# A decoder step's input projection: four items at a time, 512 prompt columns per matmul, sample tokens as the stationary operand

## The chip, the core and the metric

The program runs on one core of a Trainium2 chip. TensorE (PE) multiplies, VectorE (DVE) and ScalarE (ACT) work elementwise, GpSimd (POOL) does a few set-up operations, and SyncE (SP) issues most of the DMA transfers. The metric is the device time of one execution in microseconds. The kernel is compared with itself after one change to its first stage.

## What is computed

One decoder layer is applied to 512 prompt tokens and to 64 sample tokens (8 sequences of 8). The first stage, which the change concerns, is the RMS norm and one combined projection whose columns are then split:

```python
def mixer_inputs(x, norm_w, w_in, a_q_norm, a_k_norm):
    xn = rms_norm(x, norm_w)
    u, o, mz, ig, fg, q, kv, g, az = jnp.split(xn @ w_in, SPLIT_AT, axis=-1)
    q = rms_norm(q.reshape(B, T, A_HEADS, A_DH), a_q_norm)
    ...                       # the two key parts of kv get their own head norms
    g = jax.nn.sigmoid(g)
```

`x` has 2048 features. `u` goes through a causal convolution of four taps and a SiLU (x times its sigmoid); `o` gets a sigmoid; `z` and `az` get a SiLU; values, `o` and `z` are turned so that tokens lie on partitions. The mLSTM heads, the sparse attention of prompt and samples, the output projection and a gate follow. They are the same text in both kernels.

## The kernel before

Every stage is a block of its own, with a barrier between two stages. `project_in` is the first stage. Tokens lie on the free axis: T = 576 columns, the 512 of the prompt (TP) and then the 64 of the samples (TSA). The projection's outputs are cut into 53 **items** of 128 output features: 4 cmp, 4 key, 8 q, 1 gate, 4 val, 8 u, 8 o, 8 z, 8 az, in this order (`ITEMS`).

Each product is made of three in a rounded 32-bit type (F32R): x is split into `x_hi + x_lo`, a weight into `w_hi + w_lo`, and `w_hi·x_hi + w_hi·x_lo + w_lo·x_hi` is summed. An item has 16 contraction steps `k`. Its weights come in two halves of 8 steps (load, `w_hi` by ACT in `high`, `w_lo` by DVE in `low`, L381), in rings of three. For each step the three products are done on two column halves of 288, so an item has 96 matmuls (L250), each with its own weight load. An item's 576 columns occupy two of PSUM's banks, and three items go round in `mm`; two more banks (`aux`) serve the side work of PE.

The order on each engine is written out by hand. PE runs item s and then `aside(s - 1)`: a head norm's column sums (L218), or turns (L232). It starts item s when item s-3 has left PSUM (`evac`). On DVE, in step s: `low(2s + 2)`, `evacuate(s - 1)` (PSUM times the token's 1/rms, L417 or L408 to L410), `second(s - 2)`, `first(s - 1)`, `low(2s + 3)`. `low(m)` waits for `w_hi(m)` and for the matmuls of half m-3. ACT has `high`, the exponentials of the sigmoids (`first`, L312 to L314) and the head norms' powers (`second`). SP has the loads, and the stores of finished items.

At the start the four chunks of x arrive, ACT makes `x_hi`, DVE makes `x_lo` (L480), then ACT squares x and DVE adds the squares over `k` (L489). PE sums them over partitions behind item 1 (L257), which waits for the last addition, and ACT makes `rstd` of it. Nothing is evacuated before `rstd` is ready.

Of the kernel before, what the change touches and what calls it, by code (L numbers as in the profile page):

```python
# [14 lines left out]
P = 128  # L15
# [74 lines left out]
class Buffers:  # L90
# [3 lines left out]
ITEMS = ([("cmp", n) for n in range(4)] + [("key", n) for n in range(4)] + [("q", n) for n in range(8)] + [("gate", 0)]  # L94
         + [("val", n) for n in range(4)] + [(kind, n) for kind in ("u", "o", "z", "az") for n in range(8)])
NI = len(ITEMS)
NORMED, GATED = ("key", "q"), ("u", "o", "z", "az")
# [8 lines left out]

def project_in(nc, B, a, o):

    HALF, HK, RING = T // 2, KD // 2, 3
    STORED = ("cmp", "key", "val", "u", "az")  # L110
    halved = lambda ap: ap.rearrange("p (x t) -> p x t", x=2)
    with Semaphores(nc) as sem, ExitStack() as ctx:
        sb = lambda n, s, d=F32: ctx.enter_context(nc.sbuf_tensor(n, s, d, side="right"))
        ps = lambda n, s: ctx.enter_context(nc.psum_tensor(n, s, F32))
        xhi, xlo = sb("x_hi", [P, KD, T], F32R), sb("x_lo", [P, KD, T], F32R)
        raw = sb("w_raw", [P, RING, HK, P])
        whi, wlo = sb("w_hi", [P, RING, HK, P], F32R), sb("w_lo", [P, RING, HK, P], F32R)
        stg = sb("p_stage", [P, 3, T])
# [10 lines left out]
        mm = ps("mm", [P, 3, 2, CH])  # L129
        aux = ps("aux", [P, 2, CH])  # L130
        x_in = [sem(f"x_in{i}") for i in range(4)]
        w_in = [sem(f"w_in{i}") for i in range(RING)]
# [5 lines left out]
        whi_done, wlo_done, half_done, evac = sem("whi_done"), sem("wlo_done"), sem("half_done"), sem("evac")  # L138
# [3 lines left out]
        kv_out, row_out = [sem(f"kv_out{i}") for i in range(3)], sem("row_out")  # L142
# [5 lines left out]
        def _(sp):  # L148
            def load(m):
                if m >= 2 * NI:  # L150
                    return
                if m >= RING:
                    sp.wait_ge(wlo_done, m - RING + 1)
                sp.dma_start(raw[:, m % RING], a["w_in"][m]).then_inc(w_in[m % RING], 16)

            def store(j):
                kind, n = ITEMS[j]
                if kind in STORED:
# [6 lines left out]
                    src = stg[:, j % 3, :]  # L165
# [14 lines left out]
                    sp.dma_start(dst, src).then_inc(kv_out[j % 3], 16)  # L180
# [6 lines left out]
            for i in range(4):  # L187
                sp.dma_start(x[:, 4 * i:4 * i + 4, :], a["x_fm"][:, 4 * i:4 * i + 4, :]).then_inc(x_in[i], 16)
                if i < RING:
                    load(i)  # L190
            for s in range(NI + 2):
                load(2 * s + 3)
                load(2 * s + 4)
                if s >= 2:
                    store(s - 2)
                if 4 <= s < 4 + NB:
# [6 lines left out]
        def _(pe):  # L203
# [31 lines left out]
            for s in range(NI + 1):  # L235
# [23 lines left out]
                if s >= 1:  # L259
                    aside(s - 1)  # L260
# [2003 lines left out]
```

## Time and profile of the kernel before

| | us |
|---|---|
| median of 3 runs (2226.57 to 2228.03) | 2227.49 |
| the profiled execution | 2227.76 |
| its span from the first to the last instruction | 2226.1 |
| `project_in`, from the span's start to the next stage's first instruction | 725.5 |

In the page's busy times PE has 2051.2 us (92%), DVE 830.4 (37%), ACT 697.4 (31%), POOL 50.7 (2%). A row of the timeline gives start, length, engine, line, operation, output and inputs, the count of like instructions merged into it, and in brackets the idle time before it and what ended it. A merged row is as long as from the first start to the last end. Matmuls overlap: the distance of two starts is what one costs. So do the operations of DVE and ACT by some 0.1 us. A row of the windows gives, for a stretch, each engine's busy time with its number of instructions, then the granted TensorE clock (1.00 is 2.4 GHz, 0.50 is 1.2 GHz), the DMA share and GB/s.

### The profile page before, as it was taken

To read this page: it belongs to the slowest core of one execution; us is meant where nothing else is said; L and a number is where in the kernel's file an instruction comes from. 1 tells how busy PE (TensorE), PEld (TensorE's weight loads), DVE (VectorE), ACT (ScalarE), POOL (GpSimd) and SP (SyncE) were. 2 spreads that over 40 slices of the span, in tenths; PEclk is the share of its full clock that TensorE was granted. 3 is DMA by queue.
4 is the path that set the end of the run, shared out by engine and by line. 5 is a ranking of instruction groups with operands and counts; after the bars stand their busy time and mean duration, and the time that the engine had idled before them with its cause. 6 is when DMAs were issued, how large, how long until landed. Compare 5 with 4: busy or idle time off the path is not lost. (4 is left out here: it accounts for less than half of the span.)

```text
span 2226.1 us, 34268 instructions
## 1 busy us (share of the span) xinstructions
PE 2051.2 (92%) x13409; PEld 1658.3 (74%) x13409; DVE 830.4 (37%) x1639; ACT 697.4 (31%) x1328; POOL 50.7 (2%) x99
## 2 busy tenths in 40 slices
PE   7999999999999799968997799999997699999998
PEld 7999999999999455655554354544444599989997
DVE  6233235423332334526563134433334422242332
ACT  6332223333332222205663223332222321142222
POOL 0000000000000100000000000000000011100000
PEclk9999999999999788858998899999997799999999
DMA  5452233333331433220123768888864642223320
GB/s 190 163 187 79 87 98 98 107 102 107 99 112 53 155 140 140 82 106 29 58 75 128 262 221 277 294 298 301 301 243 152 228 147 77 81 86 107 99 73 22
DMA packets 163699, 315.00 MB, mean 142 GB/s; under 512 B 18893, under 2 KB 68430, under 8 KB 160466
## 3 DMA queue, kind: packets, MB, share of 16 engines
q1 hardware_dynamic: 143656, 278.98, 37.2%
q10 hardware_dynamic: 19882, 33.83, 4.3%
q8 instruction: 107, 1.75, 0.3%
q14 instruction: 54, 0.44, 0.1%
HBM read 280.75 MB, written 40.26 MB: 144 GB/s over the span
## 5 line engine op out<-in xcount | busy, mean ns | idle before, releaser
L250 PE MATMUL mm<-x_hi,w_hi 128*128 128x288 f32 x1696 | 368.3, 299 | 14.2 <-DVE w_lo L381 14.2
L250 PE MATMUL mm<-x_hi,w_lo 128*128 128x288 f32 x1696 | 363.9, 296 | 0.0
L250 PE MATMUL mm<-x_lo,w_hi 128*128 128x288 f32 x1696 | 363.8, 296 | 0.0
L250 PEld LDWEIGHTS mm<-x_hi,w_hi 128*128 128x128 f32 x1696 | 274.4, 189 | 15.8 <-issue 12.5
L250 PEld LDWEIGHTS mm<-x_hi,w_lo 128*128 128x128 f32 x1696 | 273.9, 189 | 0.0
L250 PEld LDWEIGHTS mm<-x_lo,w_hi 128*128 128x128 f32 x1696 | 273.8, 189 | 0.0
L381 DVE TENSOR_TENSOR w_lo<-w_raw,w_hi 128x1024 fp32r<-128x1024 f32 x106 | 129.8, 1225 | 384.8 <-ACT w_hi L280 384.8
L1515 PE MATMUL s_pH<-wide,cw_sample 128*128 128x512 f32 x512 | 244.5, 619 | 16.2 <-DMA wide<-pages 13.7
L1997 PE MATMUL o_mm<-o_feat_hi,o_w_hi 128*128 128x288 f32 x1024 | 224.7, 301 | 23.6 <-DVE o_feat_lo L2072 19.4
L1997 PE MATMUL o_mm<-o_feat_lo,o_w_hi 128*128 128x288 f32 x1024 | 221.0, 298 | 0.0
L1997 PE MATMUL o_mm<-o_feat_hi,o_w_lo 128*128 128x288 f32 x1024 | 220.7, 297 | 0.0
L280 ACT ACTIVATE w_hi<-w_raw 128x1024 fp32r<-128x1024 f32 x106 | 112.1, 1058 | 342.8 <-PE mm L250 342.7
L1515 PEld LDWEIGHTS s_pH<-wide,cw_sample 128*128 128x128 f32 x512 | 94.4, 196 | 133.3 <-issue 115.7
L1997 PEld LDWEIGHTS o_mm<-o_feat_hi,o_w_hi 128*128 128x128 f32 x1024 | 167.8, 191 | 26.3 <-issue 22.6
L1997 PEld LDWEIGHTS o_mm<-o_feat_lo,o_w_hi 128*128 128x128 f32 x1024 | 166.7, 191 | 0.0
L1997 PEld LDWEIGHTS o_mm<-o_feat_hi,o_w_lo 128*128 128x128 f32 x1024 | 166.6, 190 | 0.0
L2066 DVE TENSOR_TENSOR o_w_lo<-o_w_raw,o_w_hi 128x2048 fp32r<-128x2048 f32 x32 | 73.4, 2293 | 113.6 <-ACT o_w_hi L2027 113.6
L1753 ACT ACTIVATE s_scores<-s_scores,s_mx 128x512 f32<-128x512 f32 (+1 forms) x72 | 48.3, 671 | 115.4 <-DVE s_mx L1868 114.8
L1626 PE MATMUL s_pO<-s_kv,s_probT 128*64 128x128 f32 x1024 | 70.0, 279 | 4.7 <-DVE s_probT L1874 4.6
L1329 ACT ACTIVATE a_p<-a_pS,a_nmax 128x128 f32<-128x128 f32 (+3 forms) x128 | 66.2, 524 | 16.8 <-DVE a_nmax L1368 16.8
L2027 ACT ACTIVATE o_w_hi<-o_w_raw 128x2048 fp32r<-128x2048 f32 x32 | 60.8, 1900 | 24.3 <-DMA o_w_raw<-w_out 24.3
L1600 PE MATMUL s_pS<-s_kv,qblk 128*64 128x512 f32 x256 | 65.6, 626 | 1.1 <-DVE s_mx L1863 0.8
(402 smaller groups left out, 2296.3 us busy)
## 6 DMA issues: line engine op xcount, KB each, us to landing
wide<-pages SPq DMA_DIRECT2D x256, 256.0 KB, 3.6
w_raw<-w_in SPq DMA_DIRECT2D x106, 512.0 KB, 3.9
s_kv<-pages SPq DMA_DIRECT2D x128, 256.0 KB, 11.1
s_kv<-pages ACTq DMA_DIRECT2D x128, 256.0 KB, 8.1
o_w_raw<-w_out SPq DMA_DIRECT2D x16, 1024.0 KB, 8.6
o_w_raw<-ple_gate SPq DMA_DIRECT2D x16, 1024.0 KB, 6.7
m_state<-state SPq DMA_DIRECT2D x4, 2056.0 KB, 12.8
state_sample<-m_state SPq DMA_DIRECT2D x4, 2056.0 KB, 6.6
```

Of the source, the lines that this page charges most:

```text
L250: last = nc.tensor.matmul(mm[:, s % 3, y, 0:HALF], w[:, m % RING, kk, :], f[:, k, y * HALF:(y + 1) * HALF], start=k == 0 and i == 0, stop= ...
L280: s_.activation(whi[:, m % RING], raw[:, m % RING], ACT.Copy).then_inc(whi_done, 1)
L381: v.tensor_tensor(wlo[:, m % RING], raw[:, m % RING], whi[:, m % RING].bitcast(F32), ALU.subtract).then_inc(wlo_done, 1)
L1329: s_.activation(prob[:, d % 2, g2, 0:(qt + 1) * P], pS[:, d % 2, g2, 0:(qt + 1) * P], ACT.Exp, bias=nmx[:, d, g2:g2 + 1], accum_out=rs[:, ...
L1515: last = mm(pH[:, x, :], cw1[:, x, k, :], comp[:, HP * cc:HP * cc + HP, k * 64 + x * 32:k * 64 + x * 32 + 32], start=k == 0, stop=k == 7)
L1600: last = mm(pS[half(gp), j % 2, :], B.qblk[:, gp, b, :], kvp[:, 4 * j:4 * j + 4, gp * P:(gp + 1) * P], start=True, stop=True)
L1626: last = mm(pO[half(gp), 0, 0:P], probT[:, q % 2, i, half(gp)], kvp[:, 4 * q + i, v0:v0 + P], start=q == 0 and i == 0, stop=False)
L1753: s_.activation(chunk(j), chunk(j), ACT.Exp, bias=mx[:, 11:12], accum_out=rs[:, j:j + 1]).then_inc(p_ready, 1)
L1997: last = nc.tensor.matmul(mm[:, j % 2, x, 0:HALF], w[:, j % 2, k, :], f[:, k, cols], start=k == 0 and i == 0, stop=k == KD - 1 and i == 2)
L2027: s_.activation(whi[:, j % 2], raw[:, c % 2, :, (j % 2) * P:(j % 2 + 1) * P], ACT.Copy).then_inc(whi_done, 1)
L2066: v.tensor_tensor(wlo[:, j % 2], raw[:, (j // 2) % 2, :, (j % 2) * P:(j % 2 + 1) * P], whi[:, j % 2].bitcast(F32), ALU.subtract).then_inc( ...
```

## The change

The items stay in their order. They are grouped: `GROUPS` has 14 groups, 13 of four items and the gate alone. A group of four is done in 8 **units** of two contraction steps each, the gate in two units of eight, 106 units in all. A unit holds the weights of all four items for its two steps: 512 KB, as a half item did.

- **Prompt columns.** In a unit each of the four items has 2 steps x 3 products = 6 matmuls on all 512 prompt columns, into its own PSUM bank (`mm` has four). All four banks are finished in the group's last unit, and there is no fifth.
- **Sample columns.** The samples' x (128 stationary columns: their `x_hi` beside their `x_lo`) is loaded as weights, and the 512 output features of the group stream past it, into one bank `tail`; `w_lo` has 64 stationary columns. That is 4 matmuls of 512 columns per unit. Behind the group ACT copies `tail` to `sums` (`summed`), PE adds the two halves and turns the result back with four matmuls against `stack` (`fold`), and DVE scales the 4 x 64 columns (`sample`). The gate's samples stay moving: 48 matmuls of 64 columns.
- **Rings.** `w_hi` has three places, `w_lo` two (`LO = 2`), so `low(m)` now waits for unit m-2. The stage buffer `stg` has five places instead of three.
- **Order.** `lanes()` lays the steps of an item out over slots, one slot per unit. With `end` the slot of the group's last unit: four `prompt` at `end`, `fold` at `end + 1`, four `sample` at `end + 2`, and for item i `first` at `end + 2i + 2`, `aside` one later, `second` two later, `store` three later (six slots later still for the gate). In a slot ACT and DVE do `high(s + 2)` or `low(s + 2)` first, and then the entries, an older group's ahead of a younger one's. The convolution has moved from the evacuation to `first`.
- **Start.** `x_lo` covers the prompt alone, and DVE makes the samples' `x_lo` with a second instruction per `k`. The sum of squares on PE stands behind unit 2 and no longer behind item 1.

```diff
+GROUPS = ([[("cmp", n) for n in range(4)], [("key", n) for n in range(4)], [("q", n) for n in range(4)], [("q", n) for n in range(4, 8)],
+           [("gate", 0)], [("val", n) for n in range(4)]]
+          + [[(kind, 4 * x + n) for n in range(4)] for kind in ("u", "o", "z", "az") for x in range(2)])
...
+            def unit(m):
+                g, c = UNITS[m]
...
+                pe.wait_ge(whi_done, m + 1)
+                pe.wait_ge(wlo_done, m + 1)
+                for i in range(n):
+                    if c == 0 and g:
+                        free = start_of(g - 1) + min(i + 1, len(GROUPS[g - 1]))
+                        pe.wait_ge(prompt_out, free)
+                    own = slice(i * P, (i + 1) * P)
+                    for kk, k in enumerate(ks):
...
+                        for y, (w, x) in enumerate(((hi, xhi), (hi, xlo), (lo, xhi))):
+                            last = nc.tensor.matmul(mm[:, i, :], w[:, kk, own], x[:, k, 0:TP], start=k == 0 and y == 0, stop=k == KD - 1 and y == 2)
+                    if final:
+                        last.then_inc(item_done, 1)
...
+                        if wide:
+                            last = nc.tensor.matmul(tail[:], xhi[:, k, TP:T + TSA], hi[:, k % 2, :], start=k == 0, stop=k == KD - 1)
+                        else:
+                            last = nc.tensor.matmul(tail[0:TSA, :], xhi[:, k, TP:T], lo[:, k % 2, :], start=False, stop=False)
...
+                last.then_inc(unit_done, 1)
...
             def low(m):
...
-                if m >= RING:
-                    dve.wait_ge(half_done, m - RING + 1)
+                if m >= LO:
+                    dve.wait_ge(unit_done, m - LO + 1)
...
-            for s in range(1, NI + 2):
-                if s >= 2:
-                    low(2 * s + 2)
-                if s <= NI:
-                    evacuate(s - 1)
-                if s >= 2:
-                    second(s - 2)
-                if s <= NI:
-                    first(s - 1)
-                low(2 * s + 3)
+            for s in range(2, LAST + 1):
+                low(s + 2)
+                for what, j in LANES.get(s, []):
+                    if what == "prompt":
+                        prompt(j)
...
```

How the instructions now stand, at three places. On DVE where the last u item meets the first o item, before (L433 and L434 are the convolution, L468 the SiLU's product, L381 `low`, L417 the evacuation):

```order
L433 SCALAR_TENSOR_TENSOR p_stage<-upad,convw,p_stage 128x512 [waits p_dve_step]
L434 SCALAR_TENSOR_TENSOR p_stage<-upad,convw,p_stage 128x64
L468 TENSOR_TENSOR p_stage<-p_stage,p_square 128x576 [waits sig_ready]
L381 TENSOR_TENSOR w_lo<-w_raw,w_hi 128x1024 [waits half_done,whi_done] x2
L417 TENSOR_TENSOR p_stage<-mm,p_rstd 128x576 [waits kv_out2,half_done]
L381 TENSOR_TENSOR w_lo<-w_raw,w_hi 128x1024 [waits half_done,whi_done] x2
```

The same place of the change (L532 and L533 are the convolution of the last u item, L569 its product, L502 the prompt's evacuation, L470 `low`, L517 the samples' scaling):

```order
L532 SCALAR_TENSOR_TENSOR p_stage<-upad,convw,p_stage 128x512 [waits p_dve_step]
L533 SCALAR_TENSOR_TENSOR p_stage<-upad,convw,p_stage 128x64
L569 TENSOR_TENSOR p_stage<-p_stage,p_square 128x576 [waits sig_ready]
L502 TENSOR_TENSOR p_stage<-mm,p_rstd 128x512 [waits kv_out4,item_done]
L502 TENSOR_TENSOR p_stage<-mm,p_rstd 128x512 [waits kv_out0,item_done]
L502 TENSOR_TENSOR p_stage<-mm,p_rstd 128x512 [waits kv_out1,item_done]
L502 TENSOR_TENSOR p_stage<-mm,p_rstd 128x512 [waits kv_out2,item_done]
L470 TENSOR_TENSOR w_lo<-w_raw,w_hi 128x1024 [waits unit_done,whi_done] x2
L517 TENSOR_TENSOR p_stage<-p_turned,p_rstd 128x64 [waits fold_done] x4
```

The four evacuations of a group stand together, behind the convolution of an item of the group before and behind that slot's `low`.

On PE between two items before, with the head norm's sums between them:

```order
L250 MATMUL mm<-x_hi,w_lo 128x288 x2
L218 MATMUL aux<-p_square,p_pair 128x288 [waits sq_ready,aux_read]
L218 MATMUL aux<-p_square,p_pair 128x288
L250 MATMUL mm<-x_hi,w_hi 128x288 [waits evac,wlo_done,whi_done]
L250 MATMUL mm<-x_hi,w_hi 128x288
```

On PE between two groups of the change, the last unit of the one and the first matmuls of the next:

```order
L302 MATMUL mm<-x_hi,w_lo 128x512
L317 MATMUL p_tail<-w_lo,x_hi 64x512 x2
L315 MATMUL p_tail<-w_hi,x_hi 128x512 x2
L302 MATMUL mm<-x_hi,w_hi 128x512 [waits prompt_out,wlo_done,whi_done]
L302 MATMUL mm<-x_lo,w_hi 128x512
```

The wait `evac` was for an item three back; `prompt_out` is for the group that ended on the row above. At the end of that first unit, before the second:

```order
L302 MATMUL mm<-x_hi,w_lo 128x512
L315 MATMUL p_tail<-w_hi,x_hi 128x512 [waits sums_ready]
L315 MATMUL p_tail<-w_hi,x_hi 128x512
L317 MATMUL p_tail<-w_lo,x_hi 64x512 x2
L281 MATMUL p_turned<-p_stack,p_sums 128x64 [waits evac,sums_ready]
L281 MATMUL p_turned<-p_stack,p_sums 128x64 x3
L302 MATMUL mm<-x_hi,w_hi 128x512 [waits wlo_done,whi_done]
```

The four matmuls of L281, each 64 columns of full 32-bit, have come onto PE's queue, once per group of four.

## Rows read from the trace of the kernel before

**Rows 1.** Windows: busy time and count per engine, granted clock, DMA share.
```profile
12.40:16.50 4.10, 4.00 (x17) 4.04 (x18) 4.10 (x6) 3.33 (x5) 0.00 (x0) 1.00 0.88 324
...
40.00:718.70 678.70, 676.83 (x5055) 673.40 (x5054) 235.01 (x335) 209.98 (x262) 0.00 (x0) 1.00 0.34 108
718.70:725.50 6.80, 0.00 (x0) 0.00 (x0) 1.40 (x2) 2.05 (x3) 0.01 (x1) 0.85 0.11 43
725.50:732.00 6.50, 0.00 (x0) 0.00 (x0) 4.85 (x10) 2.05 (x3) 5.64 (x22) 0.50 0.83 297
732.00:737.00 5.00, 4.92 (x6) 2.19 (x7) 4.79 (x7) 0.60 (x1) 0.00 (x0) 0.50 1.05 346
```

**Rows 2.** Timeline of PE, two rows 17 contraction steps apart.
```profile
687.98 0.43 PE L250 MATMUL mm<-x_hi,w_hi 128*128 128x288 f32 x2
...
701.59 0.42 PE L250 MATMUL mm<-x_hi,w_hi 128*128 128x288 f32 x2
```

**Rows 3.** Timeline in the next stage: full 32-bit matmuls of 512 and 64 columns.
```profile
737.63 0.19 PEld L686 LDWEIGHTS m_pj<-m_ch,m_qkv_w 128*128 128x128 f32 x1 [0.24 <-issue]
738.06 0.19 PEld L686 LDWEIGHTS m_pj<-m_ch,m_qkv_w 128*128 128x128 f32 x1 [0.24 <-issue]
...
741.49 1.90 PE L694 MATMUL m_nm<-m_ch,m_qkv_w 128*128 128x64 f32 x16
```

**Rows 4.** Timeline of DVE around one u item.
```profile
340.11 1.23 DVE L381 TENSOR_TENSOR w_lo<-w_raw,w_hi 128x1024 fp32r<-128x1024 f32 x1 [2.55 <-ACT w_hi L280]
341.25 0.45 DVE L408 TENSOR_TENSOR upad<-mm,p_rstd 128x288 f32<-128x288 f32 x1
...
341.91 0.22 DVE L410 TENSOR_TENSOR upad<-mm,p_rstd 128x64 f32<-128x64 f32 x1
342.27 0.55 DVE L430 TENSOR_SCALAR p_stage<-upad,convw,convb 128x512 f32<-128x512 f32 x1
...
348.17 0.76 DVE L468 TENSOR_TENSOR p_stage<-p_stage,p_square 128x576 f32<-128x576 f32 x1 [2.18 <-ACT p_square L314]
```

**Rows 5.** Timeline of DVE: `second` of a q item, and of an o item.
```profile
152.35 0.57 DVE L453 SCALAR_TENSOR_TENSOR qblk<-p_stage,qnw,p_rk 64x64 f32<-64x64 f32 x2
152.94 0.75 DVE L455 SCALAR_TENSOR_TENSOR landing<-p_stage,qnw,p_rk 128x512 f32<-128x512 f32 x1
...
431.52 0.68 DVE L461 COPY p_rows<-aux 128x512 f32<-128x512 f32 x1
432.12 0.27 DVE L462 COPY p_rows<-aux 64x128 f32<-64x128 f32 x1
```

**Rows 6.** Timeline of the start, DVE's rows.
```profile
8.25 3.01 DVE L480 SCALAR_TENSOR_TENSOR x_lo<-landing,normw,x_hi 128x576 fp32r<-128x576 f32 x4 [6.54 <-ACT x_hi L349]
11.18 1.22 DVE L381 TENSOR_TENSOR w_lo<-w_raw,w_hi 128x1024 fp32r<-128x1024 f32 x1
...
19.28 1.22 DVE L381 TENSOR_TENSOR w_lo<-w_raw,w_hi 128x1024 fp32r<-128x1024 f32 x1
...
37.73 1.22 DVE L381 TENSOR_TENSOR w_lo<-w_raw,w_hi 128x1024 fp32r<-128x1024 f32 x1
```

**Rows 7.** The same start on PE: its first matmul, and the sum of squares.
```profile
12.49 0.82 PE L250 MATMUL mm<-x_hi,w_hi 128*128 128x288 f32 x2 [12.49 <-DVE w_lo L381]
...
40.09 1.13 PE L257 MATMUL aux<-p_rk,ones 128*128 128x288 f32 x4
```

**Rows 8.** Timeline of all engines at the end of `project_in`.
```profile
718.12 0.42 PE L250 MATMUL mm<-x_hi,w_lo 128*128 128x288 f32 x2
...
718.58 0.76 DVE L417 TENSOR_TENSOR p_stage<-mm,p_rstd 128x576 f32<-128x576 f32 x1 [9.09 <-PE mm L250]
719.37 0.68 ACT L312 ACTIVATE p_square<-p_stage 128x576 f32<-128x576 f32 x1 [10.68 <-DVE p_stage L417]
...
722.30 0.32 SPq L180 DMA_DIRECT2D az_scratch<-p_stage  x1
725.49 0.34 SPq L621 DMA_DIRECT2D m_qkv_w<-m_w  x1
```

More of the change, by code:

```diff
@@ L104, in nth, with lanes, put @@
     return sum(1 for kind, _ in ITEMS[:j + 1] if kind in kinds)
-def project_in(nc, B, a, o):
-    HALF, HK, RING = T // 2, KD // 2, 3
+def lanes():
+    at = {}
+    def put(slot, what, j):
+        at.setdefault(slot, []).append((what, j))
+    base = 0
+    for g, group in enumerate(GROUPS):
+        end = max(v for v, (x, _) in enumerate(UNITS) if x == g)
+        gate = group[0][0] == "gate"
+        for i in range(len(group)):
+            put(end, "prompt", base + i)
+        if not gate:
+            put(end + 1, "fold", g)
+            for i in range(len(group)):
+                put(end + 2, "sample", base + i)
+        for i in range(len(group)):
+            x = end + 2 * i + (8 if gate else 0)
+            put(x + 2, "first", base + i)
+            put(x + 3, "aside", base + i)
+            put(x + 4, "second", base + i)
+            put(x + 5, "store", base + i)
+        base += len(group)
+    return at
+def project_in(nc, B, a, o):
+    RAW, HI, LO, SLOTS = 3, 3, 2, 5
+    LANES = lanes()
+    LAST = max(LANES) + 1
+    FOLDS = [g for g, group in enumerate(GROUPS) if len(group) == 4]
+    start_of = lambda g: sum(len(group) for group in GROUPS[:g])
+    group_of = lambda j: max(g for g in range(len(GROUPS)) if start_of(g) <= j)
+    nfold = lambda g: FOLDS.index(g) + 1
     STORED = ("cmp", "key", "val", "u", "az")
-    halved = lambda ap: ap.rearrange("p (x t) -> p x t", x=2)
     with Semaphores(nc) as sem, ExitStack() as ctx:
@@ L254, in _ @@
+            for s in range(LAST + 1):
+                if s < NU:
+                    unit(s)
+                if s == 2:
                     pe.wait_ge(ones_ready, 1)
                     pe.wait_ge(added, KD - 1)
-                    for y in range(2):
-                        last = nc.tensor.matmul(aux[:, y, 0:HALF], B.ones[:], rk[:, y * HALF:(y + 1) * HALF], start=True, stop=True)
+                    for part, out in both(rk):
+                        last = nc.tensor.matmul(out, B.ones[:], part, start=True, stop=True)
@@ L357, in _ @@
                     high(3)
[L358 removed]
             act.wait_ge(ssq_done, 1)
[L360 removed]
+            for part, read in both(rstd):
+                last = s_.activation(part, read, ACT.Ln, bias=B.eps[:, 0:1], scale=1.0 / D)
+            step(last)
             s_.activation(rstd[:], rstd[:], ACT.Exp, scale=-0.5).then_inc(rs_ready, 1)
[L362 to L368 removed]
+            for s in range(2, LAST + 1):
+                high(s + 2)
+                for what, j in LANES.get(s, []):
+                    if what == "fold":
+                        summed(j)
+                    elif what == "first":
+                        first(j)
+                    elif what == "second":
+                        second(j)
         @block.vector
@@ L491, in _ @@
                     low(3)
-            low(4)
             dve.wait_ge(small_in, 16 * SMALL)
```

227 lines of the change are left out of this document (134 added, 93 removed).

## The prediction

> **What bounds the kernel now.** Read the windows first [rows 1]. From 40 to 718.7 us PE is busy for 676.83 of 678.70 us at a granted clock of 1.00; DVE and ACT are busy for a third of it. So `project_in` is bound by PE alone: what lies on PE's queue is paid in full, and DVE or ACT cost nothing unless PE comes to wait for them. The other stages are untouched. Next comes the distance of two matmuls. From 687.98 to 701.59 us lie 17 contraction steps, 102 matmuls with nothing between them [rows 2]: 13.61 / 102 = 0.1334 us each. 288 columns at 2.4 GHz are 0.1200 us, so 0.0134 us of each is something else. At the start, at 1.2 GHz, two take 0.48 us: 17 in the 4.1 us of the first window [rows 1], 0.24 us each, which is just the columns.
>
> **Matmuls.** Before: 53 x 96 = 5088, x 0.1334 = 678.7 us. The change has 104 units x 28 = 2912 matmuls of 512 columns, and 48 in the gate: 2960, plus 48 of 64 columns. Columns in all hardly differ (5088 x 288 = 1.465 million, 2960 x 512 + 48 x 64 = 1.519 million); what can be won is the 0.0134 us, 2128 times fewer. No rounded 32-bit matmul of 512 columns is in the trace. Its bounds come from two sides. Upper: the excess grows with the columns, 0.1334 x 512 / 288 = 0.2372 us. Lower: a full 32-bit one goes over the array twice, and each pass of 512 columns takes 738.06 - 737.63 = 0.43 us for 1024 column times [rows 3], 0.2133 x 2 with 0.003 over: so 0.2153 us for a single pass without the excess. Between them: the excess is fixed per matmul, 0.2133 + 0.0134 = 0.2267. I take this, since at 1.2 GHz, where a matmul lasts twice as long, none of it shows, while a share of the column time would. The 48 of 64 columns take 0.112 us each: 16 of them lie in 1.90 us, 15 distances and the last one's 0.22 [rows 3]. Sum: 2960 x 0.2267 + 5.4 = 676.4 us, **-2.3 us**; by the bounds 642.7 (-36.0) or 707.5 (+28.8).
>
> **What is added on PE.** `fold` is four full 32-bit matmuls of 64 columns, two passes each: 8 x 0.112 = 0.90 us. Twelve lie between units: **+10.8 us** (the thirteenth is in the end, below). Norm sums on 512 + 64 instead of 2 x 288 columns: 2 x 0.43 + 2 x 0.112 against 4 x 0.24 (288 columns twice), +0.12 x 12 = 1.4. The gate's turn and the first value's now stand together in one slot, and the second waits until ACT has read the first, behind a `high`: some 1.5. Together **+2.9 us**.
>
> **The wait between groups.** This is the largest term. All four `mm` banks are taken until the group's last unit, so the next group's first matmul waits for `prompt` of item 0. That stands on DVE behind `low(end + 2)`, which with `LO = 2` cannot start before unit `end` is done. So the chain begins only when PE stops, and nothing covers it: the last matmul's result 0.15 us later than a next one could start (lengths of 0.29 on starts 0.13 apart [rows 8], the same latency), signal 0.04 (718.54 to 718.58 [rows 8]), `low` 1.14 (340.11 to 341.25 [rows 4]), the evacuation of 512 columns 0.69 (0.45 for 288 [rows 4], 0.76 for 576 [rows 8], by columns), signal to PE 0.09 (12.40 to 12.49 [rows 6, 7]). 2.1 us, at 13 changes of group: **+27.4 us**. The three other evacuations (0.6 us apart) are faster than PE's 1.36 us per item.
>
> Ahead of `prompt` the older group's entries stand in the same slot, all on the path: `second` of a q item 1.26 (152.35 to 152.94, and 0.67 [rows 5]) at three changes, of a key about 0.95 at one, of o or z 0.81 (0.60 + 0.21 [rows 5]) at four; four `sample`s before the gate's evacuation 0.7 (0.22 each [rows 4], overlapping); the product of a z item 0.68 (0.76 [rows 4], overlapping) at two. The changes behind the second u group and behind the first o group have the whole `first` of a u group's fourth item: convolution, three exponentials on ACT which wait for it, product: 342.27 to 348.17 and 0.68 [rows 4], 6.6 us each. Sum 3.8 + 0.95 + 3.2 + 0.7 + 1.4 + 13.2 = **+23.2 us**. At those two PE stands for 8.7 us. After 13.5 us without a matmul (718.5 to 732.0) the clock is at 0.50 and stays there for 5 us of work [rows 1]; over the first 6.8 us of idling it was 0.85 in the mean, so it had fallen within them. From a cold start 4 us passed at half speed. I take 4 us at half speed, 2 us lost, twice: **+4.0 us**. After 2 to 4 us I expect full speed.
>
> **The start.** On DVE each `k` has 512 columns (0.67) and a 64-column instruction (0.29 [rows 5]) instead of one of 0.73 (3.01 for four, overlapping [rows 6]): +0.23. The first matmul comes 4 x 0.23 = 0.9 later, at 13.4. `low(2)` now waits for unit 0 (13.4, 4 us at half speed with 9 matmuls, 19 at 0.227: 21.7), but DVE itself gets there at 19.28 + 2.8 = 22.1 only. The last addition ends 16 x 0.23 = 3.7 later, less 0.5 that DVE idled there for ACT: 37.73 [rows 6] becomes 40.9. Before, PE reached the sum of squares at 40.09 [rows 7], busy until then. Now it stands behind unit 2: 84 matmuls, 13.4 + 4 + 75 x 0.227 = 34.4. PE waits 6.5 us, and by the rows above loses 2 us more in the clock. Sum 0.9 + 6.5 + 2 = **+9.4 us**. Unit 3's weights are ready by then.
>
> **The end.** Before, from PE's last result (718.54) to the next stage (725.49) it is 6.95 us: evacuation, three exponentials and product of one item (719.37 to 722.28 = 2.91), then the store and the barrier (3.2) [rows 8]. Now: `summed` 0.65, fold 1.1, the first sample 0.3, then four az items one behind the other, since the sigmoid's buffer `sq` is free only when the product has been taken: 4 x 2.95 = 11.8, then 3.2: 17.1 us, **+10.1 us**.
>
> **Sum.** -2.3 + 10.8 + 2.9 + 27.4 + 23.2 + 4.0 + 9.4 + 10.1 = +85.5 us. The profiled execution (2227.76) becomes 2313.3, the median of 2227.49 becomes **2313 us**. Elsewhere the queues keep up, which costs nothing as long as it holds: a u item's slot on DVE is 1.1 + 6.6, more than a unit (28 x 0.227 = 6.35), but every other slot is empty but for `low`; loads (512 KB per unit, as before per half item) are issued some four units ahead.
>
> **A page against the rows.** The matmul distance at full speed has 0.0134 us over its columns [rows 2]. The Trainium skill ("TensorE: Matmul & The Clock Gate", section "Back-to-back issue gap") gives N / 2.4 + 2.5 ns for the isolated gap. By that, 288 columns would take 0.1225 us, which this trace contradicts with 0.1334; 512 would take 0.2158, and the sum would be some 2281 us.
> The same section gives a sustained 131 ns per matmul of 512 columns beside its weight load. The trace's 0.1334 at 288 columns agrees in size; that 288 columns take 0.24 at 1.2 GHz speaks against a cost without regard to columns. Its result is the rival on the fast side below.
>
> **The rivals.**
> 1. The excess vanishes at 512 columns (it was the weight load, and 0.2153 covers it). For: the full 32-bit passes have none. Against: they load weights as well and pass 64 columns in 0.112, so a load is shorter than 0.12. 2313 - 34 = 2279 us. Chance 0.28.
> 2. The excess is a share of the columns (the array is fed at 2.16 columns per ns). For: nothing at full speed excludes it. Against: 0.24 at 1.2 GHz is the columns to the digit, though a limit in feeding could hide there. 2313 + 31 = 2344 us. Chance 0.20.
> 3. The chain between groups doesn't appear, because DVE's `low` and `prompt` run ahead of the unit's end (as `prompt` alone could: it waits for its own item). Then 27.4 + 23.2 + 4.0 go: 2258 us, with rival 1 on top 2224, at the edge of no change. Against: `low(end + 2)` is ahead of it on the queue and needs the unit's last matmul. Chance 0.05, half of it with rival 1 on top.
> 4. The other side, faster: one matmul costs the same at 512 columns as at 288, since the weight load and issue are what paces PE, not the columns. 2313 - 2960 x (0.2267 - 0.1334) = 2037 us. It decides from a distance of 0.198 us downward (85.5 / 2960 = 0.029 less than mine), under the 0.2133 that 512 columns last at 2.4 GHz. Chance 0.03.
> 5. More waits than I count (half speed after the 2 to 4 us gaps too, about 11 x 2 us): 2335 us or more. Chance 0.04.
>
> My forecast has 0.40. Its own range, from the size of the gaps, is 2305 to 2322 us. The range of all reaches to rivals 1 and 2 with 3 us each: 2276 to 2347. Faster by over 0.2% (about what a measurement of this kernel can tell from no change) 0.04, within 0.02, slower 0.94.
>
> **What would show it.** In the changed profile L302 should count 24 x 104 + 48, with starts 0.227 us apart (0.215 and 0.237 are the rivals). Between groups PE idles 13 times, mostly 2.1 to 4 us, but 8.7 us behind the second u group and behind the first o group, with DVE's L502 as the releaser; the granted clock dips behind those two. PE idles about 6.5 us near 34 us until L592. `project_in` ends near 811 us. I am wrong if PE starts a group without a gap, or if the starts are outside 0.215 to 0.237.

## The result, and the profile after

The kernel with the change takes **2333.5 us** (median; 2331.9 to 2335.2), the kernel before, on the same chip, 2227.8 (2226.6 to 2230.7): ratio 1.0475, interval 1.0462 to 1.0489. The forecast was 2313, slower, with a range of 2276 to 2347. The direction and the range held; the forecast's own range (2305 to 2322) did not, by 11.5 us. The profiled execution has a span of 2330.8 us against 2226.1.

`project_in` ends at 833.46 us instead of 725.49: +108.0. The rest of the program is 3.3 us shorter (1497.3 against 1500.6; over all kernels below it lies between 1496.2 and 1502.5, and in no order that follows their edits). So the whole question lies in `project_in`.

The page of the changed kernel, busy time and the costliest groups (line, engine, operation, tiles, count; busy us, mean ns of one; idle time before, with its releaser):

```profile
PE 2089.8 (90%) x11433; PEld 1553.9 (67%) x11433; DVE 834.1 (36%) x1694; ACT 701.3 (30%) x1354; POOL 51.2 (2%) x99
...
L302 PE MATMUL mm<-x_hi,w_hi 128*128 128x512 f32 x848 | 346.6, 409 | 63.3 <-DVE p_stage L502 35.6
```

The idle time on the row of L302 is new: 63.3 us in front of the first product of a triple, some 13 of them at the very start, and 35.6 ended by the evacuation L502 of one tile alone. The windows, with the columns of [rows 1]:

```profile
50.00:800.00 750.00, 698.71 (x3077) 559.51 (x3076) 225.73 (x344) 202.69 (x271) 0.00 (x0) 0.96 0.31 95
...
79.00:82.40 3.40, 3.40 (x10) 2.66 (x9) 0.59 (x1) 0.00 (x0) 0.00 (x0) 0.50 0.29 117
...
337.00:340.20 3.20, 0.00 (x0) 0.00 (x0) 3.10 (x6) 1.54 (x2) 0.00 (x0) 1.00 0.25 47
340.20:350.00 9.80, 9.70 (x47) 8.05 (x48) 2.97 (x4) 1.06 (x1) 0.00 (x0) 1.00 0.16 51
...
454.50:464.70 10.20, 5.25 (x12) 4.15 (x13) 4.38 (x9) 3.48 (x5) 0.00 (x0) 0.50 0.04 17
```

Against the second row of [rows 1]: where PE was idle for 1.9 of 678.7 us at a clock of 1.00, it is now idle for 51.3 of 750 at 0.96. The other rows show three of the 14 waits; the column of the clock (the last but two) tells them apart. Behind the gap at 75.5 us PE works without a pause at 0.50, 10 matmuls in 3.4 us; behind the one at 336.6, which is longer, it works at 1.00.

Two rows of PE's timeline inside a unit, 12 matmuls apart, to set beside [rows 2]:

```profile
305.00 0.39 PE L302 MATMUL mm<-x_lo,w_hi 128*128 128x512 f32 x1
...
307.72 0.39 PE L302 MATMUL mm<-x_lo,w_hi 128*128 128x512 f32 x1
```

2.72 / 12 = 0.2267 us. Over all rounded matmuls of 512 columns at full speed the middle distance is 0.227. The mean is 0.2281 without the 43 that are the first behind a wait or behind side work, which take 0.31 to 0.32.

A short gap between groups, DVE's rows and then PE's:

```profile
396.10 1.23 DVE L470 TENSOR_TENSOR w_lo<-w_raw,w_hi 128x1024 fp32r<-128x1024 f32 x1 [5.73 <-PE p_tail L315]
397.25 2.48 DVE L502 TENSOR_TENSOR upad<-mm,p_rstd 128x512 f32<-128x512 f32 x4
...
398.07 0.47 PE L302 MATMUL mm<-x_hi,w_hi 128*128 128x512 f32 x1 [2.08 <-DVE upad L502]
```

And the long one behind the second u group (the one behind the first o group reads the same, 9.05 us):

```profile
450.91 1.23 DVE L470 TENSOR_TENSOR w_lo<-w_raw,w_hi 128x1024 fp32r<-128x1024 f32 x1 [3.54 <-PE p_tail L315]
452.05 0.54 DVE L529 TENSOR_SCALAR p_stage<-upad,convw,convb 128x512 f32<-128x512 f32 x1
...
455.80 0.68 ACT L397 ACTIVATE p_square<-p_stage 128x576 f32<-128x576 f32 x1 [8.74 <-DVE p_stage L533]
...
457.94 0.76 DVE L569 TENSOR_TENSOR p_stage<-p_stage,p_square 128x576 f32<-128x576 f32 x1 [2.18 <-ACT p_square L399]
458.62 2.48 DVE L502 TENSOR_TENSOR upad<-mm,p_rstd 128x512 f32<-128x512 f32 x4
...
459.45 0.77 PE L302 MATMUL mm<-x_hi,w_hi 128*128 128x512 f32 x1 [8.64 <-DVE upad L502]
```

Nothing but `low` stands in the first chain; in the second the convolution, three exponentials and the product of the older group's fourth item stand between `low` and the evacuation that PE waits for. The order in which DVE takes them is that of [rows 4].

The start on DVE and PE, and the end on all engines:

```profile
34.43 5.93 DVE L592 TENSOR_TENSOR p_rk<-p_rk,p_stage 128x576 f32<-128x576 f32 x7
...
40.50 2.36 PE L332 MATMUL aux<-p_rk,ones 128*128 128x512 f32 x4 [5.93 <-DVE p_rk L592]
```

```profile
815.57 0.62 PE L315 MATMUL p_tail<-w_hi,x_hi 128*128 128x512 f32 x2
...
816.88 1.11 PE L281 MATMUL p_turned<-p_stack,p_sums 128*128 128x64 f32 x8 [0.69 <-ACT p_sums L364]
818.02 0.62 DVE L517 TENSOR_TENSOR p_stage<-p_turned,p_rstd 128x64 f32<-128x64 f32 x4 [2.02 <-PE p_turned L281]
818.28 0.68 ACT L397 ACTIVATE p_square<-p_stage 128x576 f32<-128x576 f32 x1 [1.45 <-DVE p_stage L517]
...
829.41 0.76 DVE L569 TENSOR_TENSOR p_stage<-p_stage,p_square 128x576 f32<-128x576 f32 x1 [2.24 <-ACT p_square L399]
...
833.46 0.33 SPq L727 DMA_DIRECT2D m_qkv_w<-m_w  x1
```

From PE's last result (815.57 + 0.62) to the next stage 17.3 us pass, against 6.95 in [rows 8].

**The clock.** The trace records the granted clock as stretches, the first of them from 16.8 us before and from 17.6 us after. (The 1.00 of the first window in [rows 1] lies ahead of that; that PE ran at 1.2 GHz there is read from the distance of 0.24 us.) Before, there was no recorded stretch at half speed up to the end of the matmuls of `project_in`; now there are eleven (us; "distance" is that of the starts of the two matmuls around the gap):

| gap begins | distance | half speed from | for | PE working in it |
|---|---|---|---|---|
| 34.2 (sum of squares) | 6.33 | 38.1 | 6.8 | 4.4 |
| 75.5 | 2.48 | 79.0 | 3.4 | 3.4 |
| 131.4 | 2.48 | none | | |
| 188.9 | 3.40 | 191.7 | 6.8 | 6.2 |
| 251.4 | 3.73 | 256.5 | 3.4 | 3.4 |
| 275.0 | 4.13 | 277.0 | 6.8 | 4.7 |
| 336.6 | 3.73 | none | | |
| 395.6 | 2.48 | none | | |
| 450.4 | 9.04 | 454.5 | 10.2 | 5.3 |
| 513.8 | 9.05 | 519.4 | 6.8 | 3.4 |
| 577.9 | 3.63 | 580.8 | 6.8 | 6.1 |
| 638.5 | 3.26 | 642.2 | 3.4 | 3.4 |
| 697.4 | 3.93 | 700.3 | 6.8 | 5.8 |
| 758.1 | 3.93 | 761.7 | 3.4 | 3.1 |

PE works 49.2 us at half speed. A matmul of 512 columns starts 0.427 us after the last there and 0.227 at full speed, so each us of this work costs 0.47 us: about 23.1 us are lost. The prediction had three such places at 2 us each.

### The profile page after: what moved, and what is told of

Read it like the earlier page. It is cut to its first block and busy times, and to the rows that moved or that the text cites. A ratio compares the mean times of both kernels' runs of the same rounds, so it can differ in the third digit from the quotient of the medians.

```text
span 2330.8 us, 30436 instructions
## 1 busy us (share of the span) xinstructions
PE 2089.8 (90%) x11433; PEld 1553.9 (67%) x11433; DVE 834.1 (36%) x1694; ACT 701.3 (30%) x1354; POOL 51.2 (2%) x99
## 5 line engine op out<-in xcount | busy, mean ns | idle before, releaser
L302 PE MATMUL mm<-x_hi,w_hi 128*128 128x512 f32 x848 | 346.6, 409 | 63.3 <-DVE p_stage L502 35.6
L302 PE MATMUL mm<-x_lo,w_hi 128*128 128x512 f32 x848 | 339.9, 401 | 0.0
L302 PE MATMUL mm<-x_hi,w_lo 128*128 128x512 f32 x848 | 339.6, 401 | 0.0
L470 DVE TENSOR_TENSOR w_lo<-w_raw,w_hi 128x1024 fp32r<-128x1024 f32 x106 | 129.9, 1225 | 508.0 <-PE p_tail L315 406.5
L1621 PE MATMUL s_pH<-wide,cw_sample 128*128 128x512 f32 x512 | 243.7, 618 | 16.8 <-DMA wide<-pages 13.9
L302 PEld LDWEIGHTS mm<-x_hi,w_hi 128*128 128x128 f32 x848 | 165.4, 195 | 101.9 <-issue 42.6
L302 PEld LDWEIGHTS mm<-x_hi,w_lo 128*128 128x128 f32 x848 | 164.9, 195 | 36.8
L302 PEld LDWEIGHTS mm<-x_lo,w_hi 128*128 128x128 f32 x848 | 165.8, 196 | 34.3
L2133 ACT ACTIVATE o_w_hi<-o_w_raw 128x2048 fp32r<-128x2048 f32 x32 | 60.8, 1900 | 23.1 <-DMA o_w_raw<-w_out 23.1
## 6 DMA issues: line engine op xcount, KB each, us to landing
m_state<-state SPq DMA_DIRECT2D x4, 2056.0 KB, 13.1
```

What stands on the lines that cost most here:

```text
L302: last = nc.tensor.matmul(mm[:, i, :], w[:, kk, own], x[:, k, 0:TP], start=k == 0 and y == 0, stop=k == KD - 1 and y == 2)
L470: v.tensor_tensor(wlo[:, m % LO], raw[:, m % RAW], whi[:, m % HI].bitcast(F32), ALU.subtract).then_inc(wlo_done, 1)
L1621: last = mm(pH[:, x, :], cw1[:, x, k, :], comp[:, HP * cc:HP * cc + HP, k * 64 + x * 32:k * 64 + x * 32 + 32], start=k == 0, stop=k == 7)
L2133: s_.activation(whi[:, j % 2], raw[:, c % 2, :, (j % 2) * P:(j % 2 + 1) * P], ACT.Copy).then_inc(whi_done, 1)
```

## The experiments

The theory is the prediction's sum with the clock's term corrected: waits between groups and what stands ahead of `prompt`, the clock behind nearly every wait, the start, the end, the fold. The rival is that the longer time comes from the matmuls themselves (a distance that grows with the columns), or from loads. Each experiment takes away one term. All but experiment 8 are made from the changed kernel.

**1. What stands ahead of the evacuation.** In a slot with evacuations DVE takes the waiting evacuation ahead of `low` and of the older group's `first`. `prompt` of item 0 needs only that item's last matmul, which comes three items before the unit's end.

```diff
             for s in range(2, LAST + 1):
-                low(s + 2)
...
+                if any(what == "prompt" for what, _ in LANES.get(s, [])):
+                    run(s, ("second", "sample", "prompt"))
+                    low(s + 2)
+                    run(s, ("first",))
+                else:
+                    low(s + 2)
+                    run(s, tuple(acts))
```

> The changed kernel with one order changed on DVE: in a group's last slot `second`, `sample` and `prompt` stand ahead of `low`, and `first` behind it. Nothing is left out. Theory A (the gap between groups is DVE's chain that starts at the unit's end, and the half-speed stretches follow from the gaps): 11 of the 13 gaps (52 us of starts' distance in all, 49 without the 0.23 of a matmul) go, the two behind u convolutions too, since the convolution moves behind `low`; project_in 108 us longer than before becomes 59, and the 49 us of work at half speed lose their 20 us besides: 2333 - 49 - 20 = 2264 us. Rival B (half speed has another cause in this stage, such as less weight loading per time): 2333 - 49 = 2284 us, with as much time at 0.50 as now. Rival C (PE waits for something else at the group's start, weights or the tail's copy): the gaps stay, 2333 us.

Measured: 2271.0 us (2268.4 to 2274.8), 1.0199 [1.0177, 1.0221]. `project_in` ends at 773.21, 60.3 us earlier. All 13 gaps between groups are gone, 52.3 us over a matmul's own distance. PE is idle for 9.2 us of 700:

```profile
50.00:750.00 700.00, 690.77 (x3124) 557.46 (x3123) 230.93 (x346) 205.12 (x274) 0.00 (x0) 0.99 0.32 102
```

A new wait came in the place of the two long ones. Rows of all engines around the first of them:

```profile
426.55 0.39 PE L302 MATMUL mm<-x_hi,w_lo 128*128 128x512 f32 x1
...
428.62 0.76 DVE L569 TENSOR_TENSOR p_stage<-p_stage,p_square 128x576 f32<-128x576 f32 x1 [2.18 <-ACT p_square L399]
429.44 0.58 ACT L364 ACTIVATE p_sums<-p_tail 128x512 f32<-128x512 f32 x1
...
430.07 0.72 PE L315 MATMUL p_tail<-w_hi,x_hi 128*128 128x512 f32 x2 [3.13 <-ACT p_sums L364]
```

PE has the next group's first prompt matmuls done and needs the bank of the sample sums, which ACT empties only behind the u item's three exponentials. 3.5 and 5.4 us there, 8.5 over the usual distance. PE's work at half speed falls from 49.2 to 15.6 us, worth 15.8. 52.3 - 8.5 + 15.8 = 59.6, for the 60.3 measured. The expectation of 2264 us didn't have the new wait and is missed by 7.

**2. Only the convolution moved.** `low` stays first, the older group's `second` too; only `first` goes behind the evacuations.

```diff
             for s in range(2, LAST + 1):
                 low(s + 2)
...
+                run(s, ("second", "sample", "prompt"))
+                run(s, ("first",))
```

> The changed kernel with `first` alone moved behind `prompt` in every slot on DVE; `low` stays ahead. It takes the convolution and SiLU (6.6 us at two changes of group) and the z product (0.7 at two) from the chain and leaves the rest. The terms of the sum: -14.6 us, so 2319 us, if half speed comes behind a 2.2 us gap as it does behind one of 8.8; some 3 us less, 2316, if it comes only behind the long ones. If the convolution were hidden anyway: 2333 us.

Measured: 2319.1 us (2316.7 to 2323.5), 1.041 [1.039, 1.0431]. The two gaps of 9.04 are 2.48 now: the older item's `first` is their difference, 6.6 us each, the prediction's term to the digit. The two gaps behind the z groups lose the product of a z item, 0.67 us each. The wait for the sample sums appears here as well (3.6 and 2.0 us) and takes back 5.1 of the 14.4:

```profile
461.31 0.58 ACT L364 ACTIVATE p_sums<-p_tail 128x512 f32<-128x512 f32 x1
...
461.94 0.76 PE L315 MATMUL p_tail<-w_hi,x_hi 128*128 128x512 f32 x2 [3.20 <-ACT p_sums L364]
```

With 47.2 us of work at half speed the clock gives back only 0.9 us, though both long gaps are gone. This already speaks against the prediction's picture, in which those two gaps and the start were the clock's only cost. 13.1 + 1.3 - 5.1 + 0.9 = 10.2; `project_in` is 9.8 us shorter.

**3. The same waits, PE kept busy.** Matmuls of 256 columns without use, into a bank that is free, fill the time in which PE would wait between groups (none before the values' group); all waits remain.

```diff
+                    g = UNITS[s][0]
+                    if s + 1 < NU and UNITS[s + 1][0] != g and FILL[g]:
...
+                        for _ in range(FILL[g]):
+                            nc.tensor.matmul(turned[:].rearrange("p i t -> p (i t)"), xhi[:, 0, 0:P], xhi[:, 0, 0:4 * TSA], start=True, stop=True)
```

> The changed kernel with useless matmuls of 256 columns put on PE between two groups (16 to 71 of them, 0.12 us each, 0.2 us shorter in all than each gap of its profile; none at the gate's), into the bank that the fold uses later. The waits between groups stay as long as they are. Theory A (idling drops the clock): the start's 6 us and the gate's gap still cost half speed, the other ten stretches go: 2333 - 16 = 2317 us, at a mean granted clock near 1.00 between 85 and 800 us. Rival B (half speed does not come from the gaps): 2333 us, the clock as now.

Measured: 2317.0 us (2314.0 to 2317.4), 1.04 [1.0381, 1.0419]. The window to set beside that of the changed kernel, and one filled gap:

```profile
50.00:800.00 750.00, 740.41 (x3524) 604.43 (x3522) 231.21 (x355) 207.32 (x278) 0.00 (x0) 1.00 0.30 96
```

```profile
443.00 8.68 PE L334 MATMUL p_turned<-x_hi 128*128 128x256 f32 x71
```

The first prompt matmul of the next group starts as late behind the fill as it did behind the idle time, at 451.82 for a `low` at 443.27, and 459.45 for 450.91 in the changed kernel: 8.55 and 8.54. Half speed is left at the start and behind the one gap not filled (it begins at 267.8 us, distance 4.13; half speed from 268.9): 7.7 us of work instead of 49.2, which is worth 19.5, and `project_in` is 20.3 shorter (the median falls by 16.5, since the rest of the program is 5.2 longer than in the changed kernel, at the upper end of its spread). **So the term that the prediction missed is the clock, and it comes from PE's idle time, not from the waits' cause.** Here the kernel whose PE does useless work through the waits is faster than the one whose PE rests.

**4. The start.** On top of experiment 1: the sum of squares stands behind unit 3 instead of unit 2, DVE and ACT split unit 4 ahead of the small work, and DVE waits for `p_rstd` only at its first evacuation.

```diff
-                if s == 2:
+                if s == 3:
                     pe.wait_ge(ones_ready, 1)
                     pe.wait_ge(added, KD - 1)
...
             def prompt(j):
                 kind, n = ITEMS[j]
+                if j == 0:
+                    dve.wait_ge(rs_ready, 1)
...
                 if k == KD // 2:
                     low(3)
+            low(4)
...
-            dve.wait_ge(rs_ready, 1)
```

> e1_ahead and a changed start: the sum of squares on PE behind unit 3 instead of unit 2, `high(4)` and `low(4)` ahead of the wait for it, and DVE's wait for `rstd` moved to the first evacuation. The prediction's term: PE's 6 us of waiting near 34 us become under 1, and the 4.4 us at half speed behind it lose their 2 us: 8 us less than e1_ahead. If the DVE's chain of additions bounds the start whatever PE does: the same time as e1_ahead.

Measured: 2265.1 us (2262.3 to 2266.7), 1.017 [1.015, 1.019], 5.9 us less than experiment 1. `project_in` is 7.1 us shorter: the wait of 6.3 is a distance of 0.53, which gives 5.8, and the clock gives 1.4; the second wait for the sample sums is 0.3 longer. The expectation had 8, with the full 2 us from the clock: the stretch at the start went, but the one behind the first wait for the sample sums grew.

**5. ACT's copy of the sample sums ahead of the SiLU.** On top of experiment 4, in the slot in which a group ends, ACT takes `summed` and only then `first` of the older item.

```diff
+                ends = any(what == "prompt" for what, _ in here) and any(what == "fold" for what, _ in after)
...
+                if ends:
+                    for what, j in after:
+                        if what == "fold":
+                            summed(j)
+                    for what, j in here:
+                        if what == "first":
+                            first(j)
```

> e4_start, and on ACT the copy of the tail (`summed`) moved ahead of the last slot's `first`. In e1_ahead and e4_start PE still waited 3.5 and 5.7 us inside the first unit behind the two u convolutions, for the tail's copy, which stood on ACT behind a `first` that waited for DVE's convolution. Theory A: both waits (9.2 us) and the 12.7 us of work at half speed behind them (6 us) go: 2265 - 15 = 2250 us, with a mean granted clock of 1.00 from 20 to 740 us. Rival: ACT's later `high` makes PE wait instead, 2258 us or more.

Measured: 2252.4 us (2250.1 to 2256.6), 1.0119 [1.01, 1.0138].

```profile
50.00:733.00 683.00, 681.93 (x3110) 550.75 (x3109) 231.19 (x348) 201.04 (x269) 0.00 (x0) 1.00 0.34 104
```

PE is idle for 1.1 of 683 us at full clock. `project_in` is 13.9 us shorter. The terms give 13.3: 8.8 of waits and 6.0 of clock, less 1.5, because at the end the older az item's SiLU now stands behind `summed` and five items are in the tail instead of four. That last point was not foreseen.

**6. The gate last.** On top of experiment 5 the gate's group of one item goes from the middle to the end, and the four SiLU items of the last az group are taken beside its matmuls.

```diff
-           [("gate", 0)], [("val", n) for n in range(4)]]
-          + [[(kind, 4 * x + n) for n in range(4)] for kind in ("u", "o", "z", "az") for x in range(2)])
+           [("val", n) for n in range(4)]]
+          + [[(kind, 4 * x + n) for n in range(4)] for kind in ("u", "o", "z", "az") for x in range(2)] + [[("gate", 0)]])
...
-            x = end + 2 * i + (8 if gate else 0)
+            x = end + (2 * i if g < len(GROUPS) - 2 else 0)
```

> e5_sums_ahead with the gate's group as the last, and the four entries of the last az group in one slot. The prediction's end term says that 17.1 us pass from PE's last unit to the next stage, of which 11.8 are four az items in a row. They now run beside the gate's second unit (8 us); and the gate's turn no longer shares a slot with a value's (1.3 us). Theory: 10 to 12 us less than e5_sums_ahead, 2239 us. If the four az items are bound by something behind PE's last unit, no change.

Measured: 2240.3 us (2238.9 to 2244.7), 1.0065 [1.0046, 1.0084]. `project_in` is 12.0 us shorter. The end, on PE and DVE:

```profile
731.64 0.28 PE L321 MATMUL p_tail<-x_hi,w_lo 128*128 128x64 f32 x1
732.29 0.76 DVE L583 TENSOR_TENSOR p_stage<-p_stage,p_square 128x576 f32<-128x576 f32 x1 [2.25 <-ACT p_square L399]
...
735.96 0.68 DVE L516 TENSOR_TENSOR grow<-mm,p_rstd 128x512 f32<-128x512 f32 x1
```

From the start of PE's last matmul of the projection (731.64) to the next stage (740.31) it is 8.7 us instead of 19.2, since two of the last four az items are done by then and the third nearly. The gate's evacuation still waits for the last one. 10.5 and the 1.3 of the gate's turn, which no longer stands beside a value's, make 11.8.

**7. The fold as single passes.** On top of experiment 6 the sums are turned by four transposes of 128 columns (one pass each), and DVE adds the two halves.

```diff
-                    last = nc.tensor.matmul(turned[:, i, :], sums[:, i * P:(i + 1) * P], stack[:], start=True, stop=True)
+                    last = nc.tensor.transpose(turned[:, i, :], sums[:, i * P:(i + 1) * P], B.ident[:])
...
+                step(v.tensor_copy(dst, fresh(lo)))
+                step(v.tensor_tensor(dst, dst, fresh(hi), ALU.add))
+                last = v.tensor_tensor(dst, dst, fresh(by), ALU.mult)
```

> e6_gate_last with the fold as four single-pass turns of 128 columns (0.109 us each in the trace) instead of four full 32-bit matmuls of 64 columns in two passes (0.90 us in all); DVE adds the two halves, three small instructions per item. It prices the term of 10.8 us by halving it: 13 x (0.90 - 0.44) = 6 us less than e6_gate_last, 2233 us. If the fold were covered by a wait of PE: the same time.

Measured: 2235.6 us (2235.3 to 2237.9), 1.004 [1.0026, 1.0054]; 4.7 us less, `project_in` 5.3 less. 52 transposes stand in the place of 104 passes; from the first of four to the next matmul it is 0.36 us instead of 0.81, 5.4 us over twelve. The group in the list by line, and the window:

```profile
L281 PE MATMUL p_turned<-ident,p_sums 128*128 128x128 f32 x52 | 7.9, 274 | 0.0
```

```profile
50.00:725.00 675.00, 675.00 (x3052) 543.90 (x3050) 256.90 (x457) 206.27 (x274) 0.00 (x0) 1.00 0.35 106
```

In this window PE does not wait at all any more, and the kernel is still 0.4% slower than before. So most of what is left is work on PE's queue, which no order removes; only the end still has a wait. Between the two `project_in` lie 9.5 us. By the distances of the starts, 4.7 are the turned sums (13 x 0.36), 2.9 the norm sums (12 times 0.997 instead of 0.754), 1.8 the prompt and sample matmuls, 0.6 the other turns and the sum of squares, 0.35 the first matmul and 1.9 the end. 0.45 of the gate's turn have moved from between the matmuls into the end. Against them stands a wait that only the kernel before has:

```profile
49.32 0.49 PE L250 MATMUL mm<-x_hi,w_hi 128*128 128x288 f32 x2 [1.72 <-DVE w_lo L381]
```

The two starts around it are 2.0 us apart, 1.9 more than usual. 4.7 + 2.9 + 1.8 + 0.6 + 0.35 + 1.9 - 0.45 - 1.9 = 9.9, for the 9.5.

**8. The kernel before with the gate last.** Its items are otherwise as they were.

```diff
-ITEMS = ([("cmp", n) for n in range(4)] + [("key", n) for n in range(4)] + [("q", n) for n in range(8)] + [("gate", 0)]
-         + [("val", n) for n in range(4)] + [(kind, n) for kind in ("u", "o", "z", "az") for n in range(8)])
+ITEMS = ([("cmp", n) for n in range(4)] + [("key", n) for n in range(4)] + [("q", n) for n in range(8)]
+         + [("val", n) for n in range(4)] + [(kind, n) for kind in ("u", "o", "z", "az") for n in range(8)] + [("gate", 0)])
```

> The kernel before with one thing changed: the gate item is the last of the 53 instead of the 17th. Its end was 6.95 us from PE's last matmul to the next stage: evacuation, three exponentials and a product of an az item, its store and the barrier. With the gate last it is evacuation 0.75, five turns 0.6, ACT's six small operations 1.7 and a barrier without a store: some 2.5 us less, 2225 us. If the barrier costs the same 3.2 us without a store: 0.5 us less, not to be told from no change.

Measured over 11 runs: 2223.8 us (2218.3 to 2226.9) against 2226.5 of the kernel before in 15: 0.9987 [0.9978, 0.9996]. `project_in` ends at 721.88, 3.6 us earlier:

```profile
718.83 0.49 PE L224 MATMUL aux<-ident,grow 64*128 64x64 f32 x5 [0.94 <-DVE grow L414]
...
721.88 0.34 SPq L621 DMA_DIRECT2D m_qkv_w<-m_w  x1
```

The gate has no store and only six short activations behind its turn, where the az item of [rows 8] has three of 576 columns, a product and a store. Of the kernels that compute the whole it is the fastest, by little.

**9. What paces a short matmul.** In the changed kernel the second and third product of each prompt triple run on 192 columns of 512. It leaves out those products for the other 320 columns; all else is as in the changed kernel.

```diff
+                            wide = TP if y == 0 else 192
+                            last = nc.tensor.matmul(mm[:, i, 0:wide], w[:, kk, own], x[:, k, 0:wide], start=k == 0 and y == 0, stop=k == KD - 1 and y == 2)
```

> The changed kernel with the second and third product of every step (w_hi with x_lo, w_lo with x_hi) on 192 of the 512 prompt columns only, so these products are missing for 320 prompt tokens. It asks what the excess over the columns is. Fixed per matmul (0.0134 us, as the 512-column distance of 0.227 said): 192 / 2.4 + 0.0134 = 0.0934 us from such a matmul to the next. A floor by the weight load at 0.112: 0.112 us. A share of the columns: 0.089 us.

One run: 2151.8 us. A triple and the next one's first matmul on PE:

```profile
230.11 0.41 PE L303 MATMUL mm<-x_hi,w_hi 128*128 128x512 f32 x1
230.36 0.25 PE L303 MATMUL mm<-x_lo,w_hi 128*128 128x192 f32 x1
230.45 0.27 PE L303 MATMUL mm<-x_hi,w_lo 128*128 128x192 f32 x1
230.56 0.42 PE L303 MATMUL mm<-x_hi,w_hi 128*128 128x512 f32 x1
```

A triple takes 0.453 us in the middle. With 0.227 for the long one, 0.113 is left for each of 192 columns, whose columns last 0.080. This is a mean: the single distances are 0.25, 0.09 and 0.11. It is close to the distance of the 64-column ones in [rows 3] (0.112) and of the transposes in experiment 7 (0.109): between 64 and 192 columns the columns hardly matter. A fixed 0.0134 on top of the columns would have given 0.413 for the triple, a share of the columns 0.415 (with 0.2372 for the long one). In the stretches at half speed a triple takes 0.853 us (268.64 to 269.49), where its columns last 0.747: with 0.427 for the long one, 0.213 is left for each short one, about twice the 0.113, so what paces them follows PE's clock. Under about 0.11 us something other than the columns paces. That it is the weight load, which 64, 128 and 192 columns all have, is the simplest reading and not shown; at 288 and 512 the 0.0134 is what is seen.

## Why the prediction came out as it did

Point by point, in the profiled execution (us; measured values from the sections above):

| term | predicted | measured |
|---|---|---|
| matmuls | -2.3 | +1.9 |
| fold, between units | +10.8 | +9.8 |
| norm sums, turns | +2.9 | +4.4 |
| waits between groups, with what stands ahead | +50.6 | +52.3 |
| clock, all places | +6.0 | +23.1 |
| start, without the clock | +7.4 | +6.9 |
| end | +10.1 | +10.4 |
| the wait before at 47 us, gone | not counted | -1.9 |
| `project_in` | +85.5 | 106.9 by the terms, 108.0 by the trace |
| the rest of the program | 0 | -3.3 |

**Matmuls: right, with a small miss.** Within a unit the distance is 0.2267, as predicted. At full speed all of them take 684.3 us, with the 48 short ones and the slower first ones behind waits and side work, against 682.4 before (0.134 each), where those 288 columns have the same surcharges that I had left out. The ends of the range, 0.2153 and 0.2372, are refuted, and with them rivals 1 and 2, which had 0.48 of the chance; so is rival 4 (0.1334 for 512 columns). The argument that chose between fixed and share was the one at 1.2 GHz, where no excess shows. It holds again here: 0.43 us pass from 460.01 to the next start at 460.44, and 512 columns last 0.427.
The Trainium skill ("TensorE: Matmul & The Clock Gate", section "Back-to-back issue gap") has N / 2.4 + 2.5 ns for an isolated matmul and a sustained 131 ns at N = 512. This trace's 226.7 ns is 11 above the first and far above the second, which holds for none of the rounded 32-bit matmuls of 512 columns here.

**Side work: right in sum.** A fold is 0.81 us instead of 0.90 (the last of its passes overlaps the next matmul). A norm sum is 0.24 longer, not 0.12: the four passes of 288 columns had taken 0.754, where I put 4 x 0.24. The gate's and the value's turn wait 1.1 longer, and the other turns are 0.5 longer in all.

**Waits between groups: right in place and size.** The base chain was put at 2.11 us and is 2.25 (2.475 less 0.227). The entries ahead of `prompt` are longer by the same pattern as predicted: the gate's samples, the q item's `second`, the u item's `first`. Experiments 1 and 2 show that these entries are the cause: with the order alone changed, the gaps go, and the 6.6 us of one `first` with them. Rival 3 is refuted in the changed kernel, and experiment 1 is what it would have looked like: 62 us less. Its 2258 did not count the wait for the sample sums, which no part of the prediction saw: `summed` stands behind ACT's exponentials. It was hidden behind the longer wait in the changed kernel and cost 8.5 us when that was gone, with the clock behind it (5.0 us for 10.7 us of work at half speed in experiment 1).

**The clock: the step that failed.** The step is "After 2 to 4 us I expect full speed". The clock fell behind eight of the eleven shorter gaps too (2.48 to 4.13 us), and behind the two long ones and the start PE worked 5.3, 3.4 and 4.4 us at half speed. 23.1 instead of 6 us: 17.1 of the 22.5 us by which `project_in` missed its sum. Rival 5 named just this, at 0.04 and 2335 us. Nothing in the rows of before excluded it. They showed a fall within 6.8 us of idling, which is a bound from above on how much idling it took, and I read it as a bound from below. The trace of before, outside those rows, spoke for rival 5. In its next stage PE idles for 2.04 and 0.78 us, and right behind it comes a stretch at half speed; the same happens at 866.8 and 918.0 us:

```profile
813.86 0.63 PE L780 MATMUL m_ht<-ident,m_shared 128*128 128x128 f32 x4 [2.04 <-ACT m_shared L894]
815.26 0.31 PE L780 MATMUL m_ht<-ident,m_shared 64*128 64x64 f32 x2 [0.78 <-ACT m_shared L894]
```

```profile
815.60:819.00 3.40, 3.40 (x4) 1.39 (x5) 0.00 (x0) 0.28 (x1) 0.00 (x0) 0.50 0.99 310
```

That the stated range held is luck. Its upper end of 2347 stood there for rival 2, which is refuted; the time came up to 2333.5 by the clock, which the sum had at 6 us. Experiment 3 settles the cause in `project_in`: same waits, PE busy, 20.3 us less.

**Start and end: right.** 6.1 us of wait for 6.5, the first matmul 0.6 later for 0.9, and 0.25 for the sum of squares in uneven parts, which I had not counted; 17.3 us of tail for 17.1. Experiments 4 and 6 take both away.

**What stays open.** Which gaps of the same size are followed by half speed and which are not (2.48 us at 75.5 yes, at 131.4 and 395.6 no; 3.73 at 251.4 yes, at 336.6 no) the rows don't tell, and with another order it falls otherwise: in experiment 2 the clock falls behind the gaps at 132 and at 335. So the clock's cost per gap can be bounded here, 0 to 2.9 us, but not forecast one by one. Idle time is not all there is to it either: in the next stage of the kernel before the clock falls at 798.5 us with no gap in PE's work, and no run here says why. Also open are the 3.3 us of the later stages and the 1.1 us between the terms and the trace.

## What to carry to other kernels

The larger groups, which share one set of accumulators, saved nothing here, since PE's time went with the columns, and they put what was a rolling handover into one point. Where a kernel does this, look up what stands on the evacuating engine's queue ahead of the evacuation that the next group needs, and on every engine that empties a bank. Price each idle gap of TensorE with the clock behind it: here 52 us of gaps between groups cost some 73, and the gaps of 2 to 4 us cost more per us than those of 9. When a gap is taken away, look for the wait that it hid before adding up the gain.

## What the hardware showed

In the changed kernel the clock fell behind 11 of 14 idle gaps of 2.25 to 8.8 us. Three of the half-speed stretches began 0.5 to 1.4 us after PE had gone back to work (half speed from 79.0, work again from 77.94), so that all 3.4 us of each were paid in work. Useless matmuls in the waits removed the stretches behind them. At full speed a rounded 32-bit matmul of 512 columns starts 0.227 us after the last, and one of 288 columns 0.134. One of 64 columns takes 0.111 (21 distances from 729.30 to 731.64 us in experiment 6), and one of 192 columns 0.113 in the mean of experiment 9.
